# Attention units' normalised tiles transposed by DMA, weights loaded by 512 KB pieces, first blocks reordered

## What is computed

```python
h = concat(meta, x)                                  # (2064, 1024) per core
for i in range(4):
    hn = rmsnorm(h, g[i])
    if i % 2 == 0:                                   # pooling layer, 4 groups of 512 channels
        u, z = split(hn @ w_in)
        t = trailing_mean(u, window) - u
        h += ((t @ w_grp) * scale * silu(z)) @ w_out
    else:                                            # GLA layer, 4 heads (dk 256, dv 512)
        q, k, v, z, glr = split(hn @ w_in)
        log_a = log_sigmoid(glr @ w_gate2 + b) / 16
        o = chunked_gated_linear_attention(q, k, v, log_a)
        h += (rmsnorm_per_head(o) * silu(z)) @ w_out
out = rmsnorm(h, final_norm)[16:]
```

## Time and profile before

| | us |
|---|---|
| runs (3): median, lowest, highest | 2003.47, 2002.89, 2023.77 |
| profiled execution: device time | 2001.86 |
| profiled execution: span of its slowest core | 2000.3 |
| busy: PE matmul, DVE, ACT, POOL | 1944.2, 1538.3, 1138.3, 252.3 |

### The profile page before, as it was taken

One profiled execution on the slowest core, in us unless ns is written; L12 is line 12 of the kernel. 1 busy time (PEld: TensorE's weight loads), 2 busy tenths in 40 slices (PEclk: granted clock), 3 DMA queues, 4 the chain that ended last, 5 costly groups with the idle time before them and its releaser, 6 DMA issues.

```text
span 2000.3 us, 55152 instructions; the slowest of 8 cores (1997.1 to 2000.3 us)
## 1 busy us (share of the span) xinstructions
PE 1944.2 (97%) x20040; PEld 1410.8 (71%) x20040; DVE 1538.3 (77%) x2848; ACT 1138.3 (57%) x2475; POOL 252.3 (13%) x396
## 2 busy tenths in 40 slices
PE   5899999999999999999999999999999999999998
PEld 3677776767767767767777777777677677677775
DVE  4868777887877777777787688788787677777888
ACT  3433323457766666667764332334776666666787
POOL 2310000011111111111221100000111111111110
PEclk9999999999999999999999999999999999999999
DMA  9522305050032031040040404050500500500011
GB/s 282 123 37 51 61 14 85 1 86 2 2 56 43 2 64 24 2 75 2 2 76 1 76 12 75 1 85 1 86 2 12 86 2 2 86 2 2 33 66 75
DMA packets 18062, 89.89 MB, mean 45 GB/s; under 512 B 2642, under 2 KB 4818, under 8 KB 9604
## 3 DMA queue, kind: packets, MB, share of 16 engines
q0 software_dynamic: 9136, 59.45, 18.0%
q1 hardware_dynamic: 8516, 26.66, 4.1%
q10 hardware_dynamic: 144, 0.26, 0.0%
HBM read 137.40 MB, written 8.39 MB: 73 GB/s over the span
## 4 chain that ended last, share of the span: by engine, by line
PE 86%; DVE 5%; ACT 4%; issue 3%; DMA 1%; DVEq 0%; ACTq 0%; SPq 0%; POOL 0%; POOLq 0%
PE ps L461 21%; PE ps L532 11%; PE ps L794 10%; PE ps L954 10%; PE ps L748 10%; PE ps L780 10%; PE ps L313 3%; PE ps L869 2%; PE ps L901 2%; PE ps L865 1%; PE ps L387 1%; DVE arena L912 1%; DMA W<-wpack 1%; DVE hnb L371 1%; DVE arena L891 1%
## 5 line engine op out<-in xcount | busy, mean ns | idle before, releaser
L461 PE MATMUL ps<-hnT,W 128*128 128x256 bf16 (+1 forms) x4096 | 465.1, 274 | 3.5 <-ACT hnT L390 2.5
L461 PEld LDWEIGHTS ps<-hnT,W 128*128 128x128 bf16 x4096 | 399.8, 98 | 68.0 <-issue 4.8
L769 POOL TENSOR_SCALAR arena<-arena 128x128 bf16<-128x128 bf16 (+1 forms) x256 | 149.7, 585 | 1021.5 <-DVE arena L891 842.5
L954 PE MATMUL ps<-W,arena 128*128 128x512 bf16 (+1 forms) x1056 | 264.0, 380 | 1.9 <-DVE arena L891 1.6
L965 DVE SCALAR_TENSOR_TENSOR h<-ps,arena,h 128x512 f32<-128x512 f32 (+1 forms) x264 | 197.9, 749 | 79.6 <-ACT arena L940 55.8
L794 PEld LDWEIGHTS ps<-hnT,W 128*128 128x128 bf16 x4224 | 241.5, 98 | 23.5 <-issue 1.3
L780 PE MATMUL ps<-W,hnT 128*128 128x512 bf16 (+1 forms) x1088 | 257.2, 379 | 0.0
L748 PE MATMUL ps<-hnT,W 128*128 128x128 bf16 (+1 forms) x4288 | 255.7, 217 | 0.0
L794 PE MATMUL ps<-hnT,W 128*128 128x128 bf16 (+1 forms) x4224 | 253.5, 218 | 0.0
L532 PE MATMUL ps<-W,arena 128*128 128x512 bf16 (+1 forms) x1088 | 248.2, 381 | 0.2 <-DVE h L536 0.2
L748 PEld LDWEIGHTS ps<-hnT,W 128*128 128x128 bf16 x4288 | 239.8, 98 | 4.1 <-issue 1.8
(11 more groups left out here) (89 smaller groups left out, 2512.0 us busy)
## 6 DMA issues: line engine op xcount, KB each, us to landing
W<-wpack POOLq DMA_DIRECT2D x53, 1024.0 KB, 16.3
h<-x SPq DMA_DIRECT2D x8, 1024.0 KB, 15.2
out<-h SPq DMA_DIRECT2D x15, 512.0 KB, 3.0
h<-wpack SPq DMA_DIRECT2D x4, 1024.0 KB, 16.3
W<-wpack POOLq DMA_DIRECT2D x7, 512.0 KB, 13.5
W<-wpack SPq DMA_DIRECT2D x3, 1024.0 KB, 17.3
gbc<-pool_norm SPq DMA_DIRECT2D x2, 512.0 KB
gbc<-gla_norm SPq DMA_DIRECT2D x2, 512.0 KB
```

Source lines behind the costliest of these rows:

```text
L461: ins = e.matmul(dst[:, f, 0:n], lhsT=Wm[:, 2 * q + f, kc, :], rhs=hnT[:, kc, c0:c0 + n], start=(kc == 0), stop=(kc == 7))
L769: P.op("pool", lambda e, dc=dc: e.tensor_scalar(out=kdT[par][:, dc, 0:n], in0=ke[par][:, dc, 0:n], scalar1=Eq[par][:, dc, n - 1:n], scalar ...
L954: ins = e.matmul(pout[0:n, :], lhsT=yT[par][:, ec, 0:n], rhs=Wo[:, ec, half * 512:(half + 1) * 512], start=(ec == 0), stop=(ec == 3))
```

## The change

- In GLA layers tiles 1 to 16 are no longer transposed by PE and copied by ACT. `scale` issues, right behind the DVE instruction, one transposing DMA from SP that reads `hnb` and writes the tile's columns of `hnT`. `step` then only counts. Tile 0 (16 rows) and all tiles of the pooling layers stay on PE, and so do the transposes of the keys (line 845).
- `load_unit` only lists pieces of 2048 columns (512 KB in SBUF, 7 or 8 per unit); `pump` issues one, once per pooling block and, in GLA, in chunks 1 to 15. The folds in the last GLA head begin one chunk later, at chunk 5.
- S of a head's chunk 0 is put behind V of the next step instead of ahead of it.
- Start of layer 0: the second half of `cast_u` goes from DVE to POOL, one output-weight cast from POOL to DVE, `prep` can split `rstd_of` into one per tile, and the steps of tiles 3 to 6 are put at other places among the matmuls.
- Final tiles 1 to 14 leave through POOL, the last two through SP and ACT, on semaphores of their own.

```diff
+    pieces = []
+    def load_unit(ui):
...
-        for p_ in parts or ((0, 2, 1, 3) if li % 2 == 0 else (0, 1, 2, 3)):
+        for p_ in (0, 2, 1, 3) if li % 2 == 0 else (0, 1, 2, 3):
             c0_, c1_ = cols[p_]
-            P.dma("pool", Wsem[s][p_], [... W[:, c0_:c1_] ...])
+            for a_ in range(c0_, c1_, 2048):
+                pieces.append((s, p_, W, src, a_))
+    def pump(reads=()):
+        if not pieces:
+            return
+        s, p_, W, src, a_ = pieces.pop(0)
+        P.dma("pool", Wsem[s][p_], [... W[:, a_:a_ + 2048] ...])
...
-        def prep(self, i):
+        def prep(self, i, split=0):
             stats_sq(i, "dve")
+            if i == 0 or split:
+                rstd_of(i, i + 1)
             if i > 0:
                 stats_sq(i + 1, "act")
-            rstd_of(i, i + (2 if i > 0 else 1))
+                rstd_of(i + split, i + 2)
         def scale(self, i):
...
+            if i > 0 and self.gla:
+                c0 = tile_col0(i)
+                P.dma("sp", s_hnt, [(lambda q: q.dma_start(out=hnT[:, :, c0:c0 + 128], in_=hnb[:, :], transpose=True), [b_hnb], [hnTb[i]])])
         def step(self, pbi, ahead=True):
...
+            if i > 0 and self.gla:
+                if ahead:
+                    self.scale(i + 1)
+                return
...
                 G["A"](0, 0)
-                G["A"](0, 1, None, step)
-                step(False)
-                norm.prep(5)
+                step()
+                G["A"](0, 1, None, lambda: step(False))
+                norm.prep(5, 1)
+                norm.scale(5)
                 G["A2"](0, 0)
-                norm.scale(5)
+                G["A"](1, 0)
+                step()
+                G["A"](1, 1, None, lambda: step(False))
+                late[0]()
                 G["A2"](0, 1)
-                G["A"](1, 0)
-                G["A"](1, 1, None, step)
-                late()
-                step(False)
                 G["A2"](1, 0)
                 G["A2"](1, 1)
+                late[1]()
+                pump()
...
-                    if 4 <= ci < 12:
-                        fold(nxt_ui, ci - 4, 4, "act")
+                    if 5 <= ci < 13:
+                        fold(nxt_ui, ci - 5, 4, "act")
...
-                if prev:
+                late_s = prev and steps[k - 1][1] == 0
+                if prev and not late_s:
                     call("S", k - 1)
                 call("Q3", k)
+                if 0 < ci < nch - 1:
+                    pump()
                 call("V", k)
+                if late_s:
+                    call("S", k - 1)
...
-    cast_u(1, "dve")
+    cast_u(1, "pool")
...
-    n0.prep(3)
+    n0.prep(3, 1)
```

More of the change, by code:

```diff
@@ L269, in build @@
     s_out2 = [P.dsem("outa"), P.dsem("outb")]
-    s_last = P.dsem("outc")
+    s_last = [P.dsem("outc%d" % i) for i in range(3)]
+    s_hnt = P.dsem("hnt")
     tile_rows = lambda i: NMETA if i == 0 else 128
@@ L289, in build @@
             units.append((li, u))
-    def load_unit(ui, parts=None):
+    pieces = []
+    def load_unit(ui):
+        assert not pieces
         li, u = units[ui]
@@ L296, in load_unit @@
         cols = {0: (0, 4096), 1: (4096, 8192), 2: (8192, 10240 if li % 2 == 0 else 12288), 3: (12288, 16384)}
-        for p_ in parts or ((0, 2, 1, 3) if li % 2 == 0 else (0, 1, 2, 3)):
+        for p_ in (0, 2, 1, 3) if li % 2 == 0 else (0, 1, 2, 3):
             c0_, c1_ = cols[p_]
-            P.dma("pool", Wsem[s][p_], [(lambda q, c0_=c0_, c1_=c1_: q.dma_start(out=W[:, c0_:c1_], in_=src[:, c0_:c1_]),
-                                         [], [Wb[s][p_]])])
+            for a_ in range(c0_, c1_, 2048):
[4 more added lines that the diff above has]
+        s, p_, W, src, a_ = pieces.pop(0)
+        P.dma("pool", Wsem[s][p_], [(lambda q: q.dma_start(out=W[:, a_:a_ + 2048], in_=src[:, a_:a_ + 2048]), list(reads), [Wb[s][p_]])])
     def fold(ui, dc, pbi, eng, halves=()):
@@ L555, in run @@
         def run(norm, before, nxt, late=None):
-            turn[0] = 3
+            turn[0] = 3 if late is not None else 2
             first = 0
@@ L994, in final_tile_b @@
                      [hb[i], b_stat[i], b_gbc], [hb[i]])
-                P.dma("sp", s_out2[i % 2], [(lambda q: q.dma_start(out=out[(i - 1) * 128:i * 128, :], in_=h[:, i, :]), [hb[i]], [])])
+                P.dma("sp" if i >= NT - 2 else "pool", s_last[2] if i >= NT - 2 else s_out2[i % 2], [(lambda q: q.dma_start(out=out[(i - 1) * 128:i * 128, :], in_=h[:, i, :]), [hb[i]], [])])
                 return
@@ L1001, in final_tile_b @@
                      [hb[i], b_stat[i], b_gbc], [b_half[z_]])
-                P.dma("act" if z_ else "sp", s_out2[z_] if z_ == i % 2 else s_last,
+                P.dma("act" if z_ else "sp", s_last[z_],
                       [(lambda q, cs=cs: q.dma_start(out=out[(i - 1) * 128:i * 128, cs], in_=h[:, i, cs]), [b_half[z_]], [])])
@@ L1208, in late_loads, with late_loads2 @@
         cast("act", W0[:, 12288:14336], hfl[:, 13 * D:15 * D], [hb[13], hb[14]], [b_wo])
-        cast("pool", W0[:, 14336:16384], hfl[:, 15 * D:17 * D], [hb[15], hb[16]], [Wb[0][3]])
+    def late_loads2():
+        cast("dve", W0[:, 14336:16384], hfl[:, 15 * D:17 * D], [hb[15], hb[16]], [Wb[0][3]])
         load_x(6, "sp")
@@ L1218, in build @@
         if li % 2 == 0:
-            run(norms[li], pending, nxt, late_loads if li == 0 else None)
+            run(norms[li], pending, nxt, (late_loads, late_loads2) if li == 0 else None)
         else:
```

## The result

| us | before | after |
|---|---|---|
| runs: median (lowest to highest) | 2004.07 (2002.89 to 2023.77, 4 runs) | 1977.66 (1976.59 to 1979.4, 4 runs) |
| profiled execution: device time, span of the slowest core | 2001.86, 2000.3 | 1976.59, 1975.0 |

The ratio of the times is 0.9857, with a 95% interval of 0.9812 to 0.9902: faster by 1.4%. The span is 25.3 us shorter; I had counted 29.4.

The account below looks back on a forecast made before the run. The prediction took PE, busy with matmuls for 97% of the span, as the bound. It summed 14.4 + 6.4 + 1.6 + 4 + 5 - 2 = 29.4 us won, forecasting 1974 us, eight-in-ten range 1963 to 2003.

Parts of the forecast that it names:

- the likeliest case: Whole program: the gains come as summed, time between 1966 and 1983 us; chance 0.62.
- PE's transposes: GLA tiles 1 to 16, two layers: 0.45 us of transposes per tile leaves PE, 14.4 us won.
- waits in bank 3 with the clock: GLA tiles: PE's waits for ACT's Exp go, 6.4 us; the lowered clock behind the second entrance's wait goes, 1.6 us.
- The entrances: Start of both GLA layers: the 4 us DMA just fits at tile 2; 2 us counted as lost.
- without that wait PE does not pause there: Second GLA entrance: with the 2.77 us wait gone PE runs on, tail matmuls keep their clock; 1.6 us won.
- The DMA: Transposing DMA of a 256 KB tile: lands in 4 us, bounds 2.2 to 13.6; hidden in 28 head-0 steps.
- S behind V: Six changes of head: V now covers S's waits of about 1 us each; 4 us won, bounds 0 and 6.0.
- First blocks: Layer 0 start: fewer PE waits for scaled tiles; 5 us won, bounds 2 us lost to 10 us won.
- Weight pieces at nothing: Weight loads in pieces on POOL: hidden, no PE wait named a weight DMA; counted at nothing.
- The DMA loop: Head 0: scaled tile, DMA, next scaled tile set the step, deciding from 9.1 us on; 2027 us, chance 0.14.
- late at the entrances: GLA entrances: a 7 us DMA loses 11 us, 1983 us, or 1988 with first blocks at zero; chance 0.12.
- PE's time did leave head 0: Against the rival that DVE and ACT's Exp hold head 0's step, so 14.4 us stay: 1988 us, chance 0.09.

Follow-up runs that it names:

- run 7: Changed kernel with the tail's four output banks taken in another order (ring start turned by two): 1971.52 us, span 1969.9.
- run 1: Changed kernel with tiles 1 to 16 of the attention layers again transposed by PE and copied by ACT: lowest 1990.95 us, profiled 1992.42, ratio 0.9922.
- run 5: Changed kernel with the first blocks of layer 0 as before (step order, whole rstd, casts on old engines; pieces stay): 1979.1 us, span 1977.6.
- run 6: Changed kernel with the output-weight cast of about 2 us back on POOL instead of DVE: 1976.19 us.
- run 4: Changed kernel with S of a head's chunk 0 ahead of V again: 1983.52 us, span 1982.0.
- run 2: Changed kernel with each unit's weights issued at once in parts of up to 1 MB, transposing DMAs kept: 2020.26 us, span 2018.7.
- run 9: Changed kernel with tail banks turned and, in the first blocks, tile 7's sum of squares and scaling moved earlier on DVE: 1970.83 us, ratio 0.9822.
- run 3: Changed kernel with each tile's transposing DMA cut into eight 128 x 128 DMAs, each waiting for the one before: 2391.61 us, span 2390.1.
- run 8: Changed kernel with the first weight piece of a layer's first head issued in chunk 4 instead of chunk 1: 1977.03 us.
- run 11: The changed kernel again, unaltered, in repeated runs: lowest 1976.23 us, profiled 1978.24, ratio to before 0.9872.

## Why the prediction was right, point by point

The forecast was 1974 us, measured were 1977.66; faster by over 1%, as the likeliest case had it. Of the 29.4 us counted 25.3 came: 1.1 too few in the first blocks, 4.7 too few in the two head 0s, and 1.7 more than counted in the other stretches. That it came so near is in part that these cancel.

- **PE's transposes, 14.4 us, and waits in bank 3 with the clock, 6.4 + 1.6 us: right in kind and size.** Steps went from 9.66 to 9.21 us, the waits for Exp left, the clock at the second entrance is 1.00. Of the 22.4 us 0.9 are tile 1 of each layer, which is transposed ahead of head 0. The 21.5 us left can be held against run 7, which has neither loss of the next point: there the two head 0s take 156.5 and 154.3 us, 20.4 less than before. Undoing the transposes cost 15.8 us (run 1), because it also undoes the losses of the next point (4.7) and because run 1 kept its clock at the second entrance (1.6). The 1.6 us were luck as a fixed term: before loses them on five cores of eight.
- **The entrances, 2 us lost: too small, and for the wrong reason.** They cost 4.7 us: 2.9 by bank and clock at layer 1 (run 7) and 1.8 by the late landing at layer 3 that goes with an instruction packet (runs 5 to 7 against after). The step that failed is "without that wait PE does not pause there": it held at the second entrance, of which it was said, but at the first, with the transposes out of the tail, attention became the next to be late, on DVE's adds. The order that I printed has attention right behind the 16 matmuls; I checked only the gate product of tile 2 against it.
- **The DMA, 4 us taken, 3.1 measured.** It is nearer to the lower bound than I took it. A transfer of 1056 packets takes 53.7% of 16 engines over 2.5 us (tile 4 in layer 3), 0.020 us for each packet, not the 0.154 of this queue's mean packet on which the 9.9 us rested; that mean came from packets of other transfers.
- **S behind V, 4 us: within the bounds.** Run 4 gives 1.0 us per change of head, the upper bound of 6 us; from before to after heads 1 and 2 show only 0.56 us each. What is late next, in layer 3, is not the state update that I named but ACT's line 942, before PE's line 888. Beyond that, plain heads of the new kernel are some 0.4 us longer than before apart from S (run 4 against before, 145.6 and 145.1 us in layer 1), also in run 2 without pieces, while PE's idle time in such a head is the same 1.0 us. Why stays open.
- **First blocks, 5 us: 3.9, in the mean of all cores 3.5, and against run 5 about 3.** DVE's 3.83 us wait for POOL before tile 3 fell to 1.22. PE's waits for scaled tiles did not shrink; of the 1.7 us of clock the slowest core of after kept all, most of its other cores not. That the cast on DVE would be what is late before tile 7 was wrong (run 6): it is the place of the sum of squares in DVE's queue, with `rstd` behind it (run 9).
- **Weight pieces at nothing: right as a cost, but half the story.** No row of PE's waits names them, yet without them the change would have been slower than before (run 2). I had looked at what they cost and not at what their absence costs the new DMA.
- **Not counted:** the 2.9 us from head 3 to layer 3. One change of head is in it, 1.1 us (524.04 us in run 4); tile 1's transposes and copy are 0.7 (523.63 in run 1); and before, PE waited 1.3 us there at line 932 for ACT's copy at 390, a row that is gone. No run takes that wait apart; it is absent from runs 1, 2, 4 and 5 too, which leaves the folds' later chunk as the likeliest cause, untested. No run undoes the final tiles' new queues either; the rest of the program, which holds them and a change of head, gained 0.6 us.
- **The rivals.** The DMA loop did not come, and run 3 shows that it would have, nearly by its own formula. Of "late at the entrances" the loss came in part, 4.7 of its 11 us and not by a landing of 7 us; the first blocks did win. PE's time did leave head 0.

The Trainium skill, "VectorE: DVE Perf Modes", section "The three transpose paths", has 1309 ns per block, on which a forecast of 2043 us would rest. The trace does not agree for a DMA of eight blocks, which lands after 3.1 us, 0.39 us per block. "Advanced Engine Details and Errata", section "X-Bar Transpose (TRN2)", was nearer: 3.1 us against the 2.2 us of 256 KB to HBM.

## What to carry to other kernels

When work leaves a stretch of an engine's queue, check every instruction behind it for what now comes too early, its bank included, and not only the one that consumes the moved result. Before handing a latency-bound transfer to the DMA engines, find what else is queued on them: here the same DMA took 3.1 us in the median and cost PE some 20 us beside 4 MB of weights. Compare a single-buffered loop (scale, transfer, scale) with the step that it must fit into; the difference times the steps gave 354 us where 379 came.

## What was not expected of the hardware

- One transposing DMA of one 128 x 128 block lands after 2.2 us (median of 256 in run 3), one of eight blocks after 3.1: 0.13 us for each of the seven more. Eight of one block that wait for each other took 18.2 to 22.6 us, 20.1 in the mean.
- One 16 KB packet of the instruction queue inside the transposing DMA of tile 3 in layer 3 goes with a landing of 4.6 to 5.2 us instead of 3.0 to 3.1, in 29 of 72 executions (nine profiles, eight cores). In other tiles it depends on when the packet comes: with nothing else beside it, DMAs landed after 3.2 us in the median where the packet started in their first 0.5 us, and after 4.4 where it started 1.5 to 2 us in. The time is that of the slowest core, and six of the nine slowest cores have the packet at tile 3.
- The length of a PE wait did not settle whether the granted clock fell. Behind waits of 1.49 to 1.86 us at these entrances it fell on no core; behind those of 2.00 to 2.05 us at attention on 34 of 48 cores (after and runs 4, 5, 6, 8 and 11); behind those of 2.70 to 2.77 us at the second entrance on five of eight cores before and on one of eight in run 1. Where it fell, 0.72 over the next 6 us on the slowest core of after, the head took about 1.5 us more, so that a wait of 2 us cost about 2 us without and 3.5 with it.
